# Experts' gates in a transformer kernel: one 256-column split product a token, one-hots scaled by ScalarE

## The reference

```python
def peer_ffn(h, w_q, keys1, keys2, u, v):
    ...
    experts = e1 * N_KEYS + e2            # 8 heads x 16 picks = 128 experts a token
    gates = jax.nn.softmax(sv, axis=-1)
    ...
    def chunk(args):
        h_c, e_c, g_c = args
        a = jnp.einsum('cd,ced->ce', h_c.astype(jnp.float32), u[e_c].astype(jnp.float32))
        act = jax.nn.gelu(a, approximate=False) * g_c
        return jnp.einsum('ce,ced->cd', act, v[e_c].astype(jnp.float32))
```

## Time and profile before

| | us |
|---|---|
| median of 3 runs (2584.11 to 2585.95) | 2585.79 |
| the profiled execution | 2584.89 |
| its span from first to last instruction | 2582.8 |
| PE busy | 2504.9 (97%) |
| POOL busy | 1713.9 (66%) |
| VectorE busy | 1486.1 (58%) |
| ScalarE busy | 674.3 (26%) |

### The profile page before, as it was taken

How to read it: one execution, slowest core, us unless ns; L and a number is a source line. 1 busy time by engine, 2 the same in 40 slices (tenths; PEclk the granted TensorE clock), 3 DMA queues, 4 the chain that set the end, 5 groups by cost and what they waited for, 6 DMA issues and landing times.

```text
span 2582.8 us, 35867 instructions
## 1 busy us (share of the span) xinstructions
PE 2504.9 (97%) x12919; PEld 2125.8 (82%) x12919; DVE 1486.1 (58%) x3290; ACT 674.3 (26%) x1215; POOL 1713.9 (66%) x1299
## 2 busy tenths in 40 slices
PE   6999999999999999999999999999999999999999
PEld 5876788888876676777788999999999978888887
DVE  7779521212413324433478897787778566666666
ACT  2137310101233424334110111111112233323332
POOL 3831476777552253474756678999997688888885
PEclk9989999999999999999999999999999999999999
DMA  9430122222221021221233348999997999999995
GB/s 381 188 114 17 50 98 98 84 98 95 88 77 49 33 71 48 82 98 66 83 121 113 127 171 300 330 336 356 366 348 271 343 368 346 352 345 352 351 350 207
DMA packets 134362, 501.85 MB, mean 194 GB/s; under 512 B 11232, under 2 KB 53600, under 8 KB 102752
## 3 DMA queue, kind: packets, MB, share of 16 engines
q1 hardware_dynamic: 70576, 311.71, 32.9%
q0 software_dynamic: 36864, 134.23, 13.7%
q10 hardware_dynamic: 26800, 54.32, 5.5%
HBM read 447.79 MB, written 52.43 MB: 194 GB/s over the span
## 4 chain that ended last, share of the span: by engine, by line
PE 74%; POOL 8%; DMA 7%; DVE 4%; issue 4%; ACT 1%; SPq 0%; ACTq 0%; DVEq 0%; POOLq 0%
PE banks L609 9%; PE banks L611 9%; PE banks L610 9%; PE banks L973 5%; PE banks L975 5%; PE banks L974 5%; PE banks L1058 3%; PE banks L1059 3%; PE banks L1060 3%; POOL W_lo L544 3%; DMA raw<-weights 3%; PE banks L778 3%; PE banks L796 2%; PE banks L1033 2%; POOL W_lo L467 2%
## 5 line engine op out<-in xcount | busy, mean ns | idle before, releaser
L492 POOL TENSOR_TENSOR W_lo<-raw,W_hi 128x512 fp32r<-128x512 f32 x376 | 495.9, 1329 | 0.0
L495 POOL TENSOR_TENSOR beat<-zero 128x1 f32<-128x1 f32 x94 | 19.2, 204 | 637.4 <-PE banks L611 208.5
L973 PE MATMUL banks<-A_hi,W_hi 128*128 128x384 f32 x1024 | 379.8, 371 | 1.1 <-issue 1.1
L975 PE MATMUL banks<-A_hi,W_lo 128*128 128x384 f32 x1024 | 345.9, 338 | 0.0
L974 PE MATMUL banks<-A_lo,W_hi 128*128 128x384 f32 x1024 | 344.3, 336 | 0.0
L467 POOL TENSOR_TENSOR W_lo<-raw,W_hi 128x2048 fp32r<-128x2048 f32 x65 | 299.6, 4609 | 5.2
L609 PE MATMUL banks<-A_hi,W_hi 128*128 128x512 f32 x680 | 268.4, 395 | 4.9 <-issue 4.9
L611 PE MATMUL banks<-A_hi,W_lo 128*128 128x512 f32 x680 | 265.6, 391 | 0.0
L610 PE MATMUL banks<-A_lo,W_hi 128*128 128x512 f32 x680 | 265.4, 390 | 0.0
L487 POOL CAST W_hi<-raw 128x512 fp32r<-128x512 f32 x376 | 248.3, 675 | 0.0
L2057 DVE TENSOR_TENSOR A_lo<-arena,A_hi 128x768 fp32r<-128x768 f32 x64 | 136.9, 2140 | 164.8 <-ACT A_hi L1498 164.7
(11 more groups left out here) (315 smaller groups left out, 5982.9 us busy)
## 6 DMA issues: line engine op xcount, KB each, us to landing
raw<-weights SPq DMA_DIRECT2D x221, 1024.0 KB, 4.9
gelu_dram<-B_plain ACTq DMA_DIRECT2D x64, 384.0 KB
gates_dram<-arena ACTq DMA_DIRECT2D x48, 512.0 KB, 10.3
arena<-gelu_dram SPq DMA_DIRECT2D x32, 768.0 KB, 8.4
arena<-gates_dram SPq DMA_DIRECT2D x30, 768.0 KB, 11.1
arena<-weights SPq DMA_DIRECT2D x15, 1024.0 KB, 10.2
B_lo_plain<-weights SPq DMA_DIRECT2D x5, 1024.0 KB, 21.0
B_plain<-weights SPq DMA_DIRECT2D x4, 1024.0 KB, 17.8
```

The lines of the kernel that those rows point to most:

```text
L492: return pool.tensor_tensor(W_lo[:, j, cols], raw[:, j, cols], W_hi[:, j, cols].bitcast(F32), ALU.subtract)
L973: mm(to, lh, rh, start=k == 0, stop=False)
L975: last = mm(to, ll, rh, start=False, stop=k == KD - 1)
```

## The change

The product of a token becomes one fp32r product of 256 columns: the first one-hot (exact in fp32r) against the second one-hot scaled by the gate's high part (128 columns) and by its low part (128 columns). The two halves of the result have to be added.

- VectorE compares four tokens at a time (GROUP): `plain_hot` writes 128x512 into a PSUM bank (0 or 1), `first_hot` writes 128x512 into SBUF. Both read the iota from SBUF now (it is copied into `ident_r`), and the token numbers from SBUF as before.
- ScalarE scales the second one-hot from PSUM into SBUF, twice a token (`scaled`), and copies the low half of the results, two tokens at a time, into `g_stage` (`low_out`). VectorE then adds the high half from PSUM (`gates_out`). In the last block VectorE sums both halves with one reduction, and ScalarE copies nothing.
- A PSUM bank holds two tokens' results now. PE waits, at each even token j, until `gates_out` of tokens j-4 and j-3 is done.
- Of 40 slabs (those behind slab 18 up to 58) the high part is written by ScalarE (`slab_high`), ahead of the gelus, in place of POOL.
- All gelu stores from slab 18 on and all gates' stores are issued by SP. The last block's stores stand behind the gelus of the last two slabs instead of ahead of them.

The core of the diff:

```diff
+            def store_gelus(s):
+                sp.wait_ge(gelu_ready, 2 * s + 2)
+                sp.dma_start(gelu_dram[s, :, :, :], gelu_out[:, 2 * (s % 2):2 * (s % 2) + 2, 0:TD])\
...
+                    store_gelus(first + s)
+                    if s < with_tokens:
...
+                            store_gates(q - 1, part)
+                    else:
+                        for part in range(STORES // 2 * (s - with_tokens), STORES // 2 * (s - with_tokens + 1)):
+                            store_gates(q, part)
...
             def split_whole(s):
+                if HOT_AT < s <= HOT_AT + HIGH_BY_ACT:
+                    pool.wait_ge(u_high, s - HOT_AT)
+                else:
...
-                            if j % 4 == 0:
-                                pe.wait_ge(g_copied, t + (GT * q + j + 4))
+                            if j % 2 == 0:
+                                pe.wait_ge(g_copied, t + (GT * q + j + 6))
+                            if j % GROUP == 0:
+                                pe.wait_ge(first_ready, t + (GT * q + j + GROUP))
                             pe.wait_ge(hot_ready, t + (GT * q + j + 1))
-                            mm(bank[4 + j // 4 % 2][:, P * (j % 4):P * (j % 4) + P], hot[j % HOTS][0],
-                               hot[j % HOTS][1], start=True, stop=True).then_inc(hot_used, 1)
+                            to = bank[4 + j // 2 % 2][:, 2 * P * (j % 2):2 * P * (j % 2) + 2 * P]
+                            mm(to.rearrange("p (h e) -> p h e", h=2), hot_first[:, j % HOTS, :],
+                               hot_second[j % HOTS], start=True, stop=True).then_inc(hot_used, 1)
...
+            def slab_high(w):
+                act.wait_ge(slab_loaded[w % 2], (w - w % 2) * 8 + 16)
+                act.wait_ge(slab_used, w - 1)
+                act.activation(W_hi[:, w % 2, :], raw[:, w % 2, :], ACT.Copy).then_inc(u_high, 1)
...
+                if isinstance(s, int) and U_AT <= s < U_AT + HIGH_BY_ACT:
+                    slab_high(N_MID + s + 1)
...
+            def scaled(group, parts):
+                act.wait_ge(plain_ready, group + 1)
+                for i in parts:
+                    t = GROUP * group + i
+                    second, plain = hot_second[t % HOTS], bank[group % 2][:, P * i:P * i + P]
+                    act.wait_ge(hot_used, t + 1)
+                    act.activation(second[:, 0, :], plain, ACT.Copy, scale=picks_t[:, 2, t:t + 1])
+                    act.activation(second[:, 1, :], plain, ACT.Copy, scale=gate_low[:, t:t + 1]).then_inc(hot_ready, 1)
+            def low_out(t):
...
+                act.wait_ge(hot_used, t + 2 + HOTS)
+                both = bank[4 + t // 2 % 2][:, :].rearrange("p (t h e) -> p h e t", t=2, h=2)
+                act.activation(stage_of(q)[:, :, j:j + 2], both[:, 1, :, :], ACT.Copy).then_inc(low_copied, 1)
...
+                        for pair in range(2):
+                            if group + 1 < TD // GROUP:
+                                scaled(group + 1, range(2 * pair, 2 * pair + 2))
+                            if q < GB - 1:
+                                low_out(GROUP * group + 2 * pair)
...
+            def plain_hot(group):
+                if group >= 2:
+                    dve.wait_ge(hot_ready, GROUP * (group - 1))
+                to = bank[group % 2][:, :].rearrange("p (t e) -> p t e", t=GROUP)
+                dve.tensor_tensor(to, *compared(group, 1), ALU.is_equal).then_inc(plain_ready, 1)
+            def first_hot(group):
+                dve.wait_ge(hot_used, GROUP * group + GROUP)
+                slot = GROUP * group % HOTS
+                dve.tensor_tensor(hot_first[:, slot:slot + GROUP, :], *compared(group, 0), ALU.is_equal)\
...
-            for t in range(TD - GT):
-                one_hot(t - t % HOTS, t % HOTS)
-                if (t + 1) * DOTS // DOT_TOKENS > k:
-                    dot(k)
-                    k += 1
+            for group in range(TD // GROUP):
+                plain_hot(group)
+                due = min(SLOTS, GROUP * (group + 1) * DOTS // DOT_TOKENS)
+                if group >= 2:
+                    gates_out(GROUP * (group - 2))
+                if due > k:
+                    dot(k)
+                    k += 1
+                if group >= 2:
+                    gates_out(GROUP * (group - 2) + 2)
+                first_hot(group)
+                if due > k:
+                    dot(k)
+                    k += 1
```

More of the change, by code:

```diff
@@ L56 @@
 U_GOT, V_GOT = 6, 8
+GROUP = 4
+HIGH_BY_ACT = KD * 5
 STORES = 8
@@ L406, in _ @@
                     load_ada(s)
-            tail = (base - N_ADA) % 2
-            with sp.Fori(LOADED_FIRST, base - N_ADA - tail - 1, 2) as s:
+            ahead = N_MID + U_AT + 3
+            assert (ahead - LOADED_FIRST) % 2 == 0
+            with sp.Fori(LOADED_FIRST, ahead - 1, 2) as s:
                 for j in range(2):
@@ L1445, in _ @@
             act.drain().then_inc(g_copied, 8)
[L1446 to L1453, removed]
+            act.activation(hot_first[:, 4:7, :], picks_t[:, 2, :].rearrange("p (i t) -> p i t", i=3), ACT.Copy)\
+                .then_inc(gate_high, 1)
@@ L1456, in _ @@
             for q, (with_tokens, between) in enumerate(U_BLOCKS):
-                if q >= 2:
-                    act.wait_ge(g_stored[q % 2], 16 * STORES * (q // 2))
-                stage = g_stage[:, q % 2, :].rearrange("p (e t) -> p e t", t=GT)
                 per_half = GT // (2 * with_tokens)
                 def tokens(half):
[L1464 to L1469, removed]
+                    for i in range(per_half // GROUP):
+                        group = (GT * q + per_half * half) // GROUP + i
+                        for pair in range(2):
[3 more added lines that the diff above has]
+                                low_out(GROUP * group + 2 * pair)
@@ L2010, in _, with compared, gates_out @@
             stage_end()
-            def one_hot(t, j):
-                dve.wait_ge(hot_used, t + (j + 1))
-                e1, e2, gate = (picks_t[:, i, bass.ds(t + j, 1)] for i in range(3))
-                dve.tensor_scalar(hot[j][0], iota_psum, e1, None, ALU.is_equal)
-                dve.tensor_scalar(hot[j][1], iota_psum, e2, gate, ALU.is_equal, ALU.mult)\
-                    .then_inc(hot_ready, 1)
+            iota_sb = ident_r[:, :].bitcast(F32)
+            def compared(group, i):
+                return (iota_sb.unsqueeze(1).to_broadcast([P, GROUP, KEYS]),
+                        picks_t[:, i, GROUP * group:GROUP * group + GROUP].unsqueeze(2).to_broadcast([P, GROUP, KEYS]))
+            def plain_hot(group):
[7 more added lines that the diff above has]
+                dve.tensor_tensor(hot_first[:, slot:slot + GROUP, :], *compared(group, 0), ALU.is_equal)\
+                    .then_inc(first_ready, GROUP)
+            def gates_out(t):
+                q, j = t // GT, t % GT
+                out_ = stage_of(q)[:, :, j:j + 2]
+                both = bank[4 + t // 2 % 2][:, :].rearrange("p (t h e) -> p e t h", t=2, h=2)
+                if q == GB - 1:
+                    if j == 0:
+                        dve.wait_ge(g_stored[q % 2], 16 * STORES * (q // 2))
+                    dve.wait_ge(hot_used, t + 2 + HOTS)
+                    dve.tensor_reduce(out_, both, AX, ALU.add).then_inc(g_copied, 2)
+                else:
+                    dve.wait_ge(low_copied, t // 2 + 1)
+                    dve.tensor_tensor(out_, out_, both[:, :, :, 0], ALU.add).then_inc(g_copied, 2)
             def dot(k):
@@ L2026, in _ @@
             dve.wait_ge(rows_ready, 1)
+            dve.wait_ge(gate_high, 1)
+            dve.tensor_tensor(gate_low.rearrange("p (i t) -> p i t", i=3), picks_t[:, 2, :].rearrange("p (i t) -> p i t", i=3),
+                              hot_first[:, 4:7, :].bitcast(F32), ALU.subtract)
+            step(dve.tensor_copy(ident_r[:, :], iota_psum))
             k = 0
[L2028 to L2030 removed]
+            for group in range(TD // GROUP):
[4 more added lines that the diff above has]
+                if due > k:
                     dot(k)
                     k += 1
[L2033 to L2035 removed]
+                if group >= 2:
[4 more added lines that the diff above has]
+                    k += 1
+            for t in range(TD - 2 * GROUP, TD, 2):
+                gates_out(t)
             def product_of(p):
```

78 lines of the change are left out of this document (50 added, 28 removed).

## The result

The changed kernel takes 2693.96 us (median of 4 runs, 2692.88 to 2700.99) against 2585.87 us of the kernel before on the same chip: 1.042 times, 95% interval 1.040 to 1.044. That is 108 us slower. Forecast were 2652 us (+68), with a range of 2575 to 2705. The sign and the two mechanisms hold. The time came out 42 us above the forecast, and these 42 us lie in three places: some 23 in the slabs with 8 tokens, 15 in the last block, 4 at the entry.

The account below looks back on a forecast made before the run. PE, busy 97%, was taken to bound the kernel. Token slabs +56, last block +6, entry +3 and exit +3 made 68 us on 2584.9: about 2652 us, range 2575 to 2705.

Parts of the forecast that it names:

- the two mechanisms: Slabs with tokens: PE's third token waits for the slab's own first gather; compares wait for POOL's subtraction.
- A token's price: On PE, a token falls from 0.24 to 0.12 us, a slab with 8 tokens from 10.3 to 9.28.
- The gather's chain: In four of five slabs PE's third token waits for the first gather behind that slab's split: 10.6 us a slab.
- Compares under POOL's subtraction: VectorE's compares, both operands in SBUF, wait for POOL's 4.6 us subtraction: median near 0.7 us, maximum above 4.
- The walk through two slabs: Token slabs alternate: a long one of 12.8 or 14.0 us, then 9.3 to 9.8; 11.0 to 11.9 a slab.
- the 11.8 a slab: Length taken for slabs with 8 tokens, nearest to the walk; against 10.4 over 40 slabs, +56 us.
- The last block: Slabs with 16 tokens, no dots: a subtraction holds one compare; 13.6 us against 12.1, +6, bounds -7 to +10.
- Entry: Before the first token, the gate's parts and first group stand in line: about +3 us, bounds 0 to +5.
- Behind the token slabs: Exit: later gates' stores on SP delay v's first gather and POOL's next subtraction: +3 us, bounds 0 to +8.
- PE-bound: Rival: gathers land early enough or VectorE is let through, so PE stays the limit: 2540 us, chance 0.16.
- Only the gather's chain: Rival: compares slip around the subtraction; token slabs take 10.6 us, about 2593 in all, chance 0.16.

Follow-up runs that it names:

- the clean kernel: Changed kernel, compares reading the iota from PSUM, plain one-hots of odd groups in SBUF, of even groups in PSUM bank 1: 2625.5 us, 1.014.
- the run with the dots where the change puts them: Changed kernel with POOL's subtraction of a slab cut into four pieces of 512 columns, nothing else changed: 2693.3 us, 1.040.

## Why the prediction was right, and where its sizes were off

- **A token's price.** Right: slabs without a stall take 9.28 us, as forecast from two starts, and 10.24 (10.21 to 10.23 measured) with 16 tokens.
- **The gather's chain.** Right as a mechanism (its count of the gathers is that of the program: those behind the split of slab n end with number 16n//5 + 4): dots one group later take 60 us off the change and 73 off the clean kernel. Its price was forecast as 10.6 a slab; alone it takes 11.41. The stalls fit (56.3 of idle in 39 slabs is 1.44 a slab, forecast 10.6 - 9.28 = 1.3); the rest is 26.6 us by which PE's instructions are longer, at a clock of 0.96.
- **Compares under POOL's subtraction.** Right: forecast were a median near 0.7 and a maximum above 4, measured 0.69 and 5.06. The rule of the Trainium skill that was weighed there (SBUF — State Buffer, Terms: exclusive lock for a full instruction) agrees with the 43 compares that start within a whole subtraction and end 0.55 to 0.56 us behind it; a compare kept waiting across four back-to-back instructions is more than it says.
- **The walk through two slabs.** The pattern is right in the main: short slabs of 9.3 and long ones of 12.4 to 16.2, where 12.8 to 14.0 was forecast. They don't alternate strictly: 25 of 39 are long, and their stalls are shorter (3.1 us on average, where the walk had 3.5 or 4.7). The term that was mis-sized is the 11.8 a slab. It contained 2.5 of stalls; measured are 78.2/39 = 2.0, less, so that 11.8 came near to 12.43 partly by luck. What it lacked is PE's longer instructions, 44.4/39 = 1.14 a slab, of which 39 us are the clock: in 19 of the 39 slabs PE runs at the half level for a time behind its stall. 9.28 + 2.0 + 1.14 = 12.43. Every stall was priced at full clock, though the forecast kept "1.00" from the stretches of a kernel that never stalled. Of the 42 us by which the total was missed, this stage has 23: 44 us of longer instructions that were not priced, less some 20 of stalls that were priced too high.
- **The last block.** Failed: forecast +6, bounds -7 to +10, measured +21. The step was "holds one compare for up to 4.6" beside an average of VectorE's work. Each of the four slabs has one compare of about 5 us, nothing lies in hand between it and PE, and ScalarE's first scalings come on top. PE, then VectorE, then ScalarE in the first of them:

```profile
2078.66 0.34 PE L1022 MATMUL banks<-A_hi,W_lo 128*128 128x384 f32 x1
2084.03 0.58 PE L1083 MATMUL banks<-A_lo,hot_first 128*128 128x256 f32 x1 [5.03 <-ACT A_hi L1516]
...
2078.30 5.01 DVE L2089 TENSOR_TENSOR banks<-ident_r,arena 128x512 f32<-128x512 f32 x1
...
2083.34 0.37 ACT L1515 ACTIVATE A_hi<-banks,arena 128x128 fp32r<-128x128 f32 x1 [4.95 <-DVE banks L2089]
2083.61 0.36 ACT L1516 ACTIVATE A_hi<-banks,tab 128x128 fp32r<-128x128 f32 x1
```

  So a slab has 5.05 idle (20.2/4) and 2.1 of longer instructions ((49.5 - 41.0)/4, at a clock of 0.83) on top of 10.24. Where the chain of compare, scaling and product is only one group deep, a sum of busy times is no upper bound.
- **Entry.** Measured +6.8, outside the forecast's bounds (+3, 0 to 5): PE's idle time grows from 2.9 to 5.6 us, as forecast (+2.7), and its busy time from 13.8 to 17.9 although its tokens are cheaper, at a clock of 0.71 instead of 1.00 (before: 16.69 us, busy 13.79; after: 23.50, 17.87). What failed is again that no price was put on PE's longer instructions. **Behind the token slabs**: +3.2, forecast +3: right in size. The first gather of v waits 5.1 us for the gates' stores instead of 3.36, and PE waits 9.1 us for VectorE's split product at the start of the value stage instead of 4.4; no run separates what share of this the place of the stores has.
- **ScalarE** is busy 8.3 us a slab (322.5/39), within the forecast 7.4 to 8.9. A scaling has 0.38 to 0.40 us in its record instead of 0.28, but neighbours start 0.25 apart.
- **The rivals.** PE-bound was priced at 2540; with both causes taken away 2546.7 to 2552.5 were measured. Its condition was wrong: the prediction asked for early gathers *or* a VectorE that is let through, but either cause alone is enough to exclude it (2625.5 with VectorE let through, 2634.5 with no wait for gathers). It needed both. "Only the gather's chain" was priced at 2593; it is 2625.5, mostly by PE's longer instructions (26.6 us in the 39 slabs).

## What to carry to other kernels

Halving the price of an instruction on the engine that sets the time makes every engine around it late by the same amount: look for the waits that were covered by that engine's slowness (here 80 us of gathers, a sum of VectorE that PE needs two tokens later, where one-hots could be eight tokens ahead), and for operands that moved onto a port which another engine holds for 5 us. Price a stall of PE of a few microseconds at more than its length (here 1.6 times on average, up to 2.1 times), since the clock behind it can be lower. And an experiment that removes a cause by giving up a buffer has a cause of its own: read its waits before its time.

## What the runs showed of the hardware that was not expected

- Behind an idle time of PE of 3.24 us its 384-column products start 0.32 us apart for some 6 us instead of 0.18 (clock 0.78 in that slab). Over the 39 slabs, 78.2 us of idle time came with a clock of 0.92 and 44.4 us of longer instructions; 4.9 us of idle time with 1.00 and 5.7. In the run with one plain buffer and later dots 25.8 us of idle time in 39 slabs, in 39 pieces of at most 0.71 us, left the clock at 1.00.
- The length of a stall alone doesn't decide. Of two long slabs of the changed kernel the first has 3.25 us of idle time and keeps 1.00, the second has 2.70 and 0.88:

```profile
1880.22:1893.02 12.80, 9.55 (x58) 9.24 (x57) 7.96 (x16) 8.27 (x24) 8.92 (x6) 1.00 1.00 374
1698.20:1712.07 13.87, 11.17 (x58) 10.84 (x57) 12.40 (x15) 8.25 (x23) 7.66 (x4) 0.88 0.89 340
```

- A compare of VectorE can be kept waiting not by one, but by four back-to-back instructions of POOL (5.30 us beside 4.96). Elsewhere in the same run it is let in between them, and in the run with the dots where the change puts them it never waits for more than two (at most 2.27 us).
